# A third output tile in a scores bank, and the last pair's values seven row groups into the second tile

## The reference

```python
h = rms_norm(x, g)
z = h @ w_in                      # 3712 columns: q, k, v, gates, conv inputs
ya = neighbourhood_attention(...) * silu(ag)     # 4 heads
yb = dilated_attention(...) * silu(bg)           # 6 heads
yc = conformer_conv(...) * silu(cg)              # 384 channels
return x + concatenate([ya, yb, yc], axis=-1) @ w_out
```

## Time and profile before

| what | value |
|---|---|
| time, 3 runs | 513.06 us median (511.6 to 513.33) |
| the profiled execution | 513.21 us |
| its span, first to last instruction | 511.4 us |
| mean granted TensorE clock | 0.996 |
| busy: PE, DVE, ACT, POOL | 501.6, 365.1, 275.5, 164.0 us |
| DMA moved | 97.79 MB, 191 GB/s mean |

### The profile page before, as it was taken

One profiled execution on the slowest core, in us unless ns is written; L12 is line 12 of the kernel. 1 busy time (PEld: TensorE's weight loads), 2 busy tenths in 40 slices (PEclk: granted clock), 3 DMA queues, 4 the chain that ended last, 5 costly groups with the idle time before them and its releaser, 6 DMA issues.

```text
span 511.4 us, 10279 instructions
## 1 busy us (share of the span) xinstructions
PE 501.6 (98%) x3998; PEld 401.9 (79%) x3998; DVE 365.1 (71%) x741; ACT 275.5 (54%) x531; POOL 164.0 (32%) x224
## 2 busy tenths in 40 slices
PE   8999999999999999999999999999999999999995
PEld 6888877887777778788888887878787877778883
DVE  6999978899984666521539878887999656852424
ACT  6844667664664475524425447676646646752314
POOL 0013332221143557425411333222122355663101
PEclk9999999999999999999999999999999999999998
DMA  8715889669986997999502378975999979899964
GB/s 292 308 43 132 198 210 207 132 162 204 232 215 159 236 251 168 245 237 278 159 2 82 88 163 196 214 174 102 220 219 223 226 166 266 217 243 247 203 169 164
DMA packets 55120, 97.79 MB, mean 191 GB/s; under 512 B 19872, under 2 KB 33696, under 8 KB 55072
## 3 DMA queue, kind: packets, MB, share of 16 engines
q0 software_dynamic: 19648, 62.93, 54.3%
q1 hardware_dynamic: 35136, 34.02, 23.1%
q10 hardware_dynamic: 288, 0.19, 0.1%
HBM read 84.92 MB, written 5.90 MB: 178 GB/s over the span
## 4 chain that ended last, share of the span: by engine, by line
PE 93%; DMA 4%; issue 1%; ACT 0%; DVE 0%; POOL 0%; POOLq 0%; SPq 0%; ACTq 0%; DVEq 0%
PE acc L607 22%; PE acc L608 21%; PE acc L609 21%; PE sc L718 5%; PE tp L751 4%; DMA w_lo<-w_out 3%; PE misc L782 2%; PE sc L669 2%; PE sc L607 1%; PE sc L609 1%; PE sc L608 1%; PE sc L670 1%; PE sc L671 1%; PE misc L777 1%; PE acc L647 1%
## 5 line engine op out<-in xcount | busy, mean ns | idle before, releaser
L607 PE MATMUL acc<-act_hi,w_hi 128*128 128x512 f32 x480 | 194.5, 405 | 0.1
L608 PE MATMUL acc<-act_hi,w_lo 128*128 128x512 f32 x480 | 187.7, 391 | 0.0
L609 PE MATMUL acc<-act_lo,w_hi 128*128 128x512 f32 x480 | 187.1, 390 | 0.0
L607 PEld LDWEIGHTS acc<-act_hi,w_hi 128*128 128x128 f32 x480 | 90.2, 188 | 21.9 <-issue 3.9
L609 PEld LDWEIGHTS acc<-act_lo,w_hi 128*128 128x128 f32 x480 | 90.2, 188 | 19.9
L608 PEld LDWEIGHTS acc<-act_hi,w_lo 128*128 128x128 f32 x480 | 90.3, 188 | 17.1 <-issue 0.5
L877 ACT ACTIVATE w_lo<-w_hi 128x1024 fp32r<-128x1024 f32 (+1 forms) x62 | 61.9, 999 | 47.3 <-DMA w_hi<-w_out 38.0
L1320 DVE SCALAR_TENSOR_TENSOR y<-ub,par,y 128x512 f32<-128x512 f32 x90 | 70.0, 777 | 0.0
L1092 POOL DMA_DIRECT2D w_lo<-w_in x40 | 35.9, 897 | 106.2 <-ACT w_lo L877 105.5
L1320 DVE SCALAR_TENSOR_TENSOR ub<-ub,par 128x512 f32<-128x512 f32 x84 | 63.3, 754 | 0.0
L939 ACT ACTIVATE prob<-prob,nmx 128x384 f32<-128x384 f32 (+1 forms) x80 | 45.3, 567 | 25.1 <-DVE nmx L1342 24.9
(11 more groups left out here) (150 smaller groups left out, 718.7 us busy)
## 6 DMA issues: line engine op xcount, KB each, us to landing
w_hi<-w_in POOLq DMA_DIRECT2D x40, 512.0 KB, 5.8
w_lo<-w_in POOLq DMA_DIRECT2D x40, 512.0 KB, 6.1
w_hi<-w_out POOLq DMA_DIRECT2D x16, 512.0 KB, 6.4
w_lo<-w_out POOLq DMA_DIRECT2D x16, 512.0 KB, 7.0
pT<-w_in SPq DMA_DIRECT2D x15, 512.0 KB, 5.5
v<-v_way SPq DMA_DIRECT2D x40, 112.0 KB, 5.3
v_way<-vs SPq DMA_DIRECT2D x24, 112.0 KB, 5.6
gf<-nabias SPq DMA_DIRECT2D x20, 128.0 KB, 5.5
```

Source lines behind the costliest of these rows:

```text
L607: nc.tensor.matmul(to[:, :], w_hi[:, slot, k, :], a_hi[:, k, :], start=i == 0, stop=False)
L608: nc.tensor.matmul(to[:, :], w_lo[:, slot, k, :], a_hi[:, k, :], start=False, stop=False)
L609: last = nc.tensor.matmul(to[:, :], w_hi[:, slot, k, :], a_lo[:, k, :], start=False, stop=i == K - 1)
```

## The change

The second tile (33) now runs seven groups before `values`. Then the third tile (`THIRD`, tile 34) is opened, in `sc0`, which the scores have left, and runs seven groups. Then each of the three tiles gets its last group, and tiles 35 to 39 follow as before. Tile 2 of the second layer, which uses `sc0` next, also waits for tile 34 to be read. Tile 35 still goes to `acc1`, behind tile 33.

```diff
--- before.py
+++ after.py
@@ -350,9 +350,11 @@
 
             return emptied(l - 1, N_IN + CT + k)
 
+        THIRD = N_IN + CT + 2
+
         def bank_of(c):
 
-            return sc[c % 2] if c in (2, 3) else acc[c % 2]
+            return sc[c % 2] if c in (2, 3, THIRD) else acc[c % 2]
 
         def v_tile(g):
             return IN_TILES.index(("bv", g) if g < DPAIRS else ("av", g - DPAIRS))
@@ -624,6 +626,9 @@
                     if l:
 
                         pe.wait_ge(m_ready, UNITS * l)
+                        pe.wait_ge(acc_free, emptied(l - 1, THIRD))
+                elif c == THIRD:
+                    pe.wait_ge(m_ready, UNITS * (l + 1))
                 else:
                     pe.wait_ge(acc_free, emptied(l, c - (4 if c in (4, 5) else 2)))
 
@@ -858,12 +863,14 @@
                 open_tile(l, c)
                 products(c, act_hi, act_lo, 0, KD - 1, order=K_ORDER, ready=(ylo_ready, KD * l))
                 open_tile(l, c + 1)
-                products(c + 1, act_hi, act_lo, 0, 3, order=K_ORDER)
+                products(c + 1, act_hi, act_lo, 0, KD - 1, order=K_ORDER)
                 values(l, PAIRS - 1)
-                products(c + 1, act_hi, act_lo, 3, KD - 2, order=K_ORDER)
+                open_tile(l, c + 2)
+                products(c + 2, act_hi, act_lo, 0, KD - 1, order=K_ORDER)
                 products(c, act_hi, act_lo, KD - 1, KD, order=K_ORDER, ready=(ylo_ready, KD * l))
-                products(c + 1, act_hi, act_lo, KD - 2, KD, order=K_ORDER)
-                for c in range(N_IN + CT + 2, N_CH):
+                products(c + 1, act_hi, act_lo, KD - 1, KD, order=K_ORDER)
+                products(c + 2, act_hi, act_lo, KD - 1, KD, order=K_ORDER)
+                for c in range(N_IN + CT + 3, N_CH):
                     open_tile(l, c)
                     products(c, act_hi, act_lo, order=X_ORDER[l + 1], used=act_used if c == N_CH - 1 else None)
```

## The result

| | kernel before | changed kernel |
|---|---|---|
| median | 513.07 us | 518.70 us |
| lowest to highest of 6 | 511.60 to 513.33 | 518.04 to 519.87 |
| profiled execution, span | 513.21, 511.4 us | 518.10, 516.3 us |

The ratio is 1.0121, with a 95% interval of 1.0101 to 1.0141: slower by some 5.6 us, where +3.05 was forecast. The time lies 0.1 us above the range. The direction and the place were right; the size was not.

The account below looks back on a forecast made before the run. PE was taken as the bound, with full DMA engines. Small terms put tile 35 at -0.35 us and the wait for tile 36's weights added 3.4: +3.05 us, forecast 516.1 us, range 513.6 to 518.6.

Parts of the forecast that it names:

- Small gains: First layer's output on PE: -0.32 us before `values`, -0.1 before tile 32's last group, +0.2 for tile 35's bank.
- the second term: Before tile 32's last group: tile 34's 21 steps cover the gate and splits, saving PE a wait of 0.1 us.
- The late issue: POOL's queue: `load_lo` of tile 36, behind `load_hi` of 37, goes out at 228.07 instead of 223.18.
- The flight of 9.4 us: Tile 36's second weight transfer takes 9.4 us as before, landing at 237.5, so PE waits 3.4 us.
- Tile 37 with 0.5 us to spare, no second wait: Tile 37's second transfer lands at 242.44, before its opening at 242.94, so PE does not wait again.
- the third rival: Clock falls to half during PE's wait before tile 36: +1.5 us, together 517.6 us; chance 0.18.
- a clock under 1.00 at 237: Sign in the new profile, near the end of PE's wait for tile 36, that would show the clock falling.
- The rule on a transfer's time: About 2.0 us plus bytes over 436 GB/s: tile 36's weights land at 231.3, no wait, sum -0.35 us.

Follow-up runs that it names:

- e7: Changed kernel with tile 36's second transfer issued ahead of tile 37's first and SP's raw tiles held back: 513.15 us, ratio 1.0004.
- e10: Changed kernel with three groups of the third tile ahead of tile 32's last, tile 36's second transfer ahead of tile 37's first, raw tiles held back: 513.11 us.
- e5: Changed kernel with tile 36's second transfer issued ahead of tile 37's first on POOL's queue: 517.13 us, ratio 1.0079.
- e4: Changed kernel with only three groups of the third tile ahead of tile 32's last group, its other five behind tile 33's last: 513.68 us.
- e9: Changed kernel with five groups of the third tile, instead of seven, ahead of tile 32's last group: 516.37 us, ratio 1.0066.
- e8: Kernel before, PE's order untouched, with POOL's first transfer of tile 37 waiting for tile 34's end instead of tile 32's: 518.19 us.
- e1: The changed kernel unaltered, run again for a second trace: 519.0 us, ratio 1.0104.
- e6: Changed kernel with SP's four raw tiles of the second layer's weights held back until tiles 35, 36, 37 and 37 are done: 515.27 us.
- e2: Changed kernel with 14 unused 128x128 matmuls on PE ahead of tile 36's opening: 516.99 us, ratio 1.0069.
- e3: Changed kernel with the last pair's values back behind three groups of tile 33, the third tile kept: 518.78 us, ratio 1.0107.

## Why the prediction was wrong, and where it was right

- **Small gains** (-0.32, -0.1, +0.2). `values` followed its matmul without the wait, no wait stood before tile 32's last group, and tile 35 waited 0.19 us for DVE. Right by the trace, but they don't add up as the prediction's sum has them: -0.32 - 0.1 + 0.2 is -0.22, where its times put tile 35 0.35 early. By its own rows the second term is 0.26 and not 0.1: from 219.12 to tile 35's opening at 229.00 PE took 42 steps, 9.52 us, and 0.36 over, of which 0.1 stays in the new order. e7 and e10 show that their sum can't be measured.
- **The late issue.** Predicted at 227.41 (with the 0.66 taken off), found at 227.43. e5, e4, e9 and e8 show it as the cause: issue it early and the wait goes, delay it in the old kernel and it comes.
- **The flight of 9.4 us.** Found 9.8, and 9.5 to 10.1 in e1 to e4. The argument that what slowed it is still there held: without the raw tiles it took 7.7 (e6, and 7.9 in e8, where the first ones had landed), and without tile 37's first transfer ahead of it as well 5.6 (e10). By these, each of the two cost some 2.1 us. The flight accounts for +0.4 of the error: the wait cost 3.50 instead of 3.05.
- **Tile 37 with 0.5 us to spare, no second wait.** Right, but closer: its second transfer landed at 242.5 (234.10 + 8.4), and at full clock tile 37 would have opened at 242.72 (237.28 + 5.44), 0.2 us later. In the trace the low clock made the room; in e2, at full clock, there was no wait either.
- **The step that failed** is the third rival, in these words: "It is one fall at one place, and the waiting time is close to it, so I give it 0.18 and not more." The sum put nothing for the clock. My own row said that the clock fell 2.75 us behind PE's stop, and my forecast wait was 3.3 us; the sum should have had the fall in it. The low clock was there in every trace of a wait of over 3 us (the changed kernel, e1, e3, e8) and in one of the two between 2 and 3 us (e9, not e5). Its price, put at +1.5, was 1.74 in the trace and 2.0 by e2 against e1; by tile 36's time it was also 1.74 in e1, 1.78 in e8, 1.60 in e9 and 2.90 in e3. With the rival taken as the forecast, 517.6, plus 0.4 for the flight and 0.24 for the clock's price, the sum is 518.2. The 0.5 us left to the median of 518.7 stays open: executions with a low stretch as long as e3's would account for it, but both traces of the changed kernel have the short one. The sign that the prediction gave, a clock under 1.00 at 237, would have missed the fall, which came at 238.2.
- **The rule on a transfer's time** of the Trainium skill ("DMA: Bandwidth & Descriptors", section "Anatomy of one DMA"), weighed against rows 7, gave 3.2 us for 512 KB. Tile 36's accumulating transfer does not agree: it took 5.5 us at the least (e5), with nothing issued beside it for 3.0 of them.

## What to carry to other kernels

When work is moved ahead of the end of something, ask which queue waits for that end, what stands behind the wait in that queue, and how much slack *that* has: here 1.9 us of slack stood against 4.9 us of delay, on POOL's queue, which the edit never touched. And when a wait of PE is forecast, look whether rows show the clock falling after one as long. Here it fell in all four traces with an unfilled wait of 3.4 to 3.7 us and in the one of 2.25 us, and not in the one of 2.58 us. Then put its price into the sum (1.6 to 1.8 us here, once 2.9), or give PE something to do in the wait: 14 matmuls whose result nothing reads won 2 us here. Room in a queue is cheaply made: two exchanged issues and a later prefetch took the whole loss back (e7).

## What was not expected of the hardware

- The clock can fall after the wait is over. In the changed kernel PE stopped at 233.9, resumed at 237.28, and the granted clock went down near 238.2; in e1 near 239.6 and in e8 near 239.8, more than 1 us after the return. In e9 it went down 2.0 us behind the stop, in e3 2.8. It was low for about 3.4 us in four traces and for 6.8 in e3.
- One transfer of 512 KB, the same one, took from 5.5 us (e5) to 10.1 us (e3), by what was issued just ahead of it and beside it.
